# Expert weights read in one 8 KB run per partition, and the expert loop laid out around four plus two PSUM banks

## Chip, cores and metric

The kernel runs on one core of a Trainium2 chip. The metric is the device time of one execution in microseconds (us), lower is better. TensorE (PE) does matrix products, VectorE (DVE) and ScalarE (ACT) elementwise work, GpSimd (POOL) little here, and SyncE (SP) issues the transfers, which 16 DMA engines carry out.

## What is computed

Two transformer blocks over 256 tokens of width 1024 in float32. The change touches only the mixture of experts that ends the first block:

```python
def moe_ffn(h, router_w, router_b, w_mlp1, b_mlp1, w_mlp2, b_mlp2):
    ...
    top_vals, top_idx = lax.top_k(logits, TOP_K)          # 4 of 32 experts for each token
    ...
    def expert_step(acc, params):
        w1, b1, w2, b2, gate_e = params
        u = xt @ w1 + b1                                  # w1 is 1024 x 2048
        glu = jnp.minimum(u[:, ::2], SWIGLU_LIMIT)
        lin = jnp.clip(u[:, 1::2], -SWIGLU_LIMIT, SWIGLU_LIMIT)
        a = glu * jax.nn.sigmoid(SWIGLU_ALPHA * glu) * (lin + 1)
        out = a @ w2 + b2                                 # w2 is 1024 x 1024
        return acc + gate_e[:, None] * out.astype(jnp.float32), None
```

## The kernel before

The first block has its projections, attention and output product, then `rms_modulate`, `route` and `mixture`; the second block (two layers) follows. `route` (L1640) makes a list of work items, each one expert with at most 64 of its tokens (a few with up to 96), on the device. `mixture` (L1853) takes the items two at a time; such a pair i has 128 places, 64 and 64 (`even`) or 96 and 32 (`uneven`). There are 16 pairs in this execution.

**Transfers.** A pair needs 24 pieces of 1 MB, alternately of its two experts: j = 0 to 7 are the first 1024 columns of `w_mlp1`, 8 to 15 the other 1024, 16 to 23 `w_mlp2`. A piece holds 256 rows, two for each partition, 128 rows apart: two runs of 4 KB (`moe_load`, L1632). There are 12 slots (`MOE_SLOTS`): numbers 4 to 7 are the shared weight ring of the whole kernel (`ring`), the others `moe_ring`. SP loads piece j into slot j % 12 as soon as the product that used the slot's last content has added to `halves_done` (L2216 to L2221). The first 12 pieces are loaded ahead, in `rms_modulate` and `route`. When 10 of the last pair's 12 steps are done, SP issues the next stage's first weights (`refill`).

**Products.** `products_of` (L1925) is one step: it waits for two pieces, does 8 calls of a float32 matmul (16 instructions; twice as many of half width for uneven pairs), and adds to `halves_done`. A pair is 12 steps: u for output columns 0 to 1023 in banks 0 and 1 (four steps), u for 1024 to 2047 in the same banks (four), y in the same banks (four). So each bank pair must be emptied before the next bias product (`biases`, L1919) starts it anew: by DVE (`gate`: glu and lin) after the fourth and eighth step, by ACT (copies to `moe_y`) after the twelfth.

**Between the steps** PE also does: `put_back` (L1939), which spreads the last pair's y over the tokens, for DVE to add to the residual (`add_put`); `gather` (L1902), which picks the next pair's tokens out of `turned_h` by the 0/1 matrix `sel`, for ACT to copy to `moe_x`; `turn_hidden` (L1911), which transposes the gated result (128 columns at a time) for ACT to copy to `moe_hid`; and the transpose of `gated`, for ACT to copy to `moe_back`. These use banks 2 and 3 (`misc`, `summed`). Banks 4 to 7 hold the products with b2 at the beginning (`acc`). The order is written by hand: put_first after step 4, put_second after 5, the first two turns after 6, gathers after 8 and 9, the other turns after 10, `gated` after 11. `sigmoid` runs on ACT between `gate` and `multiply` on DVE.

Of the kernel before, what the change touches and what calls it, by code (L numbers as in the profile page):

```python
# [213 lines left out]
class Builder:  # L214
# [1408 lines left out]
    def moe_piece(self, j):  # L1623

        x = j % MOE_SLOTS
        if SHARED <= x < SHARED + SLOTS:
            at = self.ring[:, x - SHARED, :, :]
        else:
            at = self.moe_more[:, x if x < SHARED else x - SLOTS, :, :]
        return at.rearrange("p a b -> p (a b)").rearrange("p (k c) -> p k c", k=2)  # L1630

    def moe_load(self, sp, j, expert):  # L1632

        g, kk = j // 8, j // 2 % 4
        name, c = ("w_mlp1", g) if g < 2 else ("w_mlp2", 0)
        w = self.dram[name][0].rearrange("e (c p) n -> e p c n", p=P)
        src = w[bass.ds(expert, 1), :, 2 * kk:2 * kk + 2, 1024 * c:1024 * c + 1024]
        sp.dma_start(self.moe_piece(j), src.rearrange("e p c n -> (e p) c n")).then_inc(self.moe_landed[j % MOE_SLOTS], 16)
# [214 lines left out]
    def mixture(self, comb_t, b2, ctx):  # L1853
# [16 lines left out]
        glu, lin, sig, act_out = (self.sb(f"moe_{n}", [P, 2, 256], ctx=ctx) for n in ("glu", "lin", "sig", "act"))  # L1870
# [9 lines left out]
        out = self.bank[0:2]  # L1880
        misc = lambda half: self.bank[2 + half][:, 0:S]
        summed = lambda d: self.bank[2 + d // 2 % 2][:, S * (d % 2):S * (d % 2) + S]
# [10 lines left out]
        with self.stage() as block:  # L1893
            @block.tensor
            def _(pe):
# [15 lines left out]
                def turn_hidden(i, q):  # L1911

                    pe.wait_ge(hidden.sem, i * 4 + (q + 1))
                    for j in range(2):
                        mm = nc.tensor.transpose(misc(q % 2)[:, PAIR * j:PAIR * j + PAIR],
                                                 act_out[:, q % 2, P * j:P * j + P], ident)
                    mm.then_inc(turned.sem, 1)

                def biases(g):  # L1919

                    for o in range(2):
                        nc.tensor.matmul(out[o][:, :], row_of[:, 2 * g + o, :], b1, start=True, stop=False,
                                         skip_group_check=True)

                def products_of(i, tiles, g, kk, lhs):  # L1925

                    for m in range(2):
                        j = 8 * g + 2 * kk + m
                        pe.wait_ge(landed[j % slots], i * (16 * chunks // slots) + 16 * (j // slots + 1))
                    for k in (2 * kk, 2 * kk + 1):  # L1930
                        for o in range(2):
                            for c, n_cols, m in tiles:
                                mm = nc.tensor.matmul(out[o][c:c + n_cols, :], lhs[:, k, c:c + n_cols],  # L1933
                                                      self.moe_piece(8 * g + 2 * kk + m)[:, k % 2, 512 * o:512 * o + 512],
                                                      start=(g == 2 and k == 0), stop=(k == KC - 1),
# [10 lines left out]
                def put_first(i):  # L1946

                    put_back(0)
# [23 lines left out]
                def pair(i, tiles, after=True):  # L1972

                    pe.wait_ge(rows_ready.sem, i + 1)
                    taken(i, 0)
                    if after:
                        pe.wait_ge(y_taken.sem, i * 2)
                    biases(0)
                    products_of(i, tiles, 0, 0, x)
                    yield  # L1980
                    for kk in (1, 2, 3):
                        products_of(i, tiles, 0, kk, x)
                        yield
                    if after:
                        put_first(i)
                    pe.wait_ge(lins.sem, i * 4 + 2)
                    biases(1)
                    products_of(i, tiles, 1, 0, x)
                    yield
                    if after:  # L1990
                        put_second(i)
# [1330 lines left out]
```

## Time and profile before

| | us |
|---|---|
| three runs | 2628.89, 2629.95, 2622.94 (median 2628.89) |
| the profiled execution | 2629.03 |
| its span, first to last instruction | 2627.2 |
| PE busy in the span | 2358.1 |
| DVE, ACT, POOL busy | 960.5, 719.2, 136.8 |

The expert loop lies from about 319 to 1294 us of the span, some 37% of it. In the page of the profile, the span is cut into 40 slices of 66 us. A line of the timeline gives the start, the duration, engine, source line, what is written <- what is read, a count, and in brackets how long the engine stood idle before it and for whom. Matmul durations overlap: a group that lasts 1.99 us is followed by the next one 1.92 us after its start. Each float32 matmul call is two records (x16 is 8 calls), a transpose one.

### The profile page before, as it was taken

What the parts mean: (1) busy time and instruction counts of PE and PEld (TensorE: products, weight loads), DVE (VectorE), ACT (ScalarE), POOL (GpSimd) and SP (SyncE); (2) the same over time, 40 slices, a digit from 0 to 9 for tenths busy, and PEclk for the clock granted to TensorE, in tenths of its full rate; (3) what the DMA queues carried; (4) which work ended last, traced back from release to release, by engine and by line L of the source; (5) the groups of instructions that cost most, each with busy time, mean ns of one, the idle gap of its engine ahead of it and who ended that gap; (6) DMA issues with size and microseconds to landing.
All of it is one profiled execution on the core that took longest, in us unless ns stands there. A gap on an engine that the chain in (4) does not pass through costs nothing. (4 is left out here: it accounts for less than half of the span.)

```text
span 2627.2 us, 37215 instructions
## 1 busy us (share of the span) xinstructions
PE 2358.1 (90%) x14984; PEld 1555.3 (59%) x14984; DVE 960.5 (37%) x1779; ACT 719.2 (27%) x1166; POOL 136.8 (5%) x145
## 2 busy tenths in 40 slices
PE   6988899999999999999899977999999989888997
PEld 4966533333333333333498555678787788557997
DVE  2355312111211111111321656654344431756565
ACT  2354211111111111111232544342122242445333
POOL 0100000000000000000000213200000200211000
PEclk9988799999999999999999988999999999989999
DMA  9655699999999999999823433232332223434462
GB/s 288 167 164 181 238 393 404 402 409 403 407 408 406 409 410 410 408 409 409 314 83 109 161 102 107 81 96 61 108 106 71 88 75 125 145 105 134 145 192 83
DMA packets 351334, 605.52 MB, mean 230 GB/s; under 512 B 15056, under 2 KB 251600, under 8 KB 351088
## 3 DMA queue, kind: packets, MB, share of 16 engines
q1 hardware_dynamic: 351216, 603.84, 63.9%
q8 instruction: 88, 1.44, 0.2%
q14 instruction: 30, 0.25, 0.0%
HBM read 602.74 MB, written 1.05 MB: 230 GB/s over the span
## 5 line engine op out<-in xcount | busy, mean ns | idle before, releaser
L1933 PE MATMUL banks<-moe_ring,moe_x 128*64 128x512 f32 (+1 forms) x1920 | 346.9, 597 | 5.5 <-DMA moe_ring<-in_w_mlp 5.4
L2136 DVE TENSOR_SCALAR moe_glu<-banks 128x256 f32<-128x256 f32 x64 | 26.9, 420 | 736.1 <-PE banks L1933 736.1
L1933 PEld LDWEIGHTS banks<-moe_ring,moe_x 128*64 128x64 f32 (+1 forms) x1920 | 104.9, 126 | 223.5 <-issue 223.5
L2533 PE MATMUL banks<-ff_xhi,ff_whi 128*128 128x512 f32 (+1 forms) x672 | 226.5, 337 | 5.5 <-PEq L235 3.9
L2533 PE MATMUL banks<-ff_xhi,ff_wlo 128*128 128x512 f32 (+1 forms) x672 | 226.2, 337 | 0.0
L2533 PE MATMUL banks<-ff_xlo,ff_whi 128*128 128x512 f32 (+1 forms) x672 | 226.1, 337 | 0.0
L529 DVE TENSOR_TENSOR ff_wlo<-ring,ff_whi 128x2048 fp32r<-128x2048 f32 (+2 forms) x76 | 152.7, 2010 | 116.1 <-ACT ff_whi L520 113.9
L803 PE MATMUL banks<-pr_whi,pr_xhi 128*128 128x256 f32 (+1 forms) x640 | 180.4, 282 | 1.2 <-DVE pr_wlo L529 1.2
L803 PE MATMUL banks<-pr_wlo,pr_xhi 128*128 128x256 f32 (+1 forms) x640 | 180.4, 282 | 0.0
L803 PE MATMUL banks<-pr_whi,pr_xlo 128*128 128x256 f32 (+1 forms) x640 | 180.3, 282 | 0.0
L520 ACT CAST ff_whi<-ring 128x2048 fp32r<-128x2048 f32 (+2 forms) x76 | 127.2, 1674 | 149.4 <-PE banks L2588 122.2
L1933 PE MATMUL banks<-ring,moe_x 128*64 128x512 f32 (+1 forms) x640 | 116.3, 596 | 40.0 <-DMA ring<-in_w_mlp 40.0
L529 DVE TENSOR_TENSOR pr_wlo<-ring,pr_whi 128x2048 fp32r<-128x2048 f32 (+1 forms) x34 | 73.7, 2166 | 191.6 <-ACT pr_whi L520 191.6
L2533 PEld LDWEIGHTS banks<-ff_xhi,ff_whi 128*128 128x128 f32 x672 | 127.7, 190 | 19.5 <-issue 4.5
L2533 PEld LDWEIGHTS banks<-ff_xhi,ff_wlo 128*128 128x128 f32 x672 | 127.7, 190 | 13.1
L2533 PEld LDWEIGHTS banks<-ff_xlo,ff_whi 128*128 128x128 f32 x672 | 127.7, 190 | 13.0
L2588 PE MATMUL banks<-ff_hid_hi,ff_whi 128*128 128x512 f32 (+1 forms) x352 | 122.4, 348 | 12.3 <-PEq L235 12.3
L1933 PE MATMUL banks<-moe_ring,moe_hid 128*64 128x512 f32 (+1 forms) x640 | 116.8, 597 | 15.8 <-DMA moe_ring<-in_w_mlp 11.9
L803 PEld LDWEIGHTS banks<-pr_whi,pr_xhi 128*128 128x128 f32 x640 | 123.1, 192 | 3.1 <-issue 1.7
L803 PEld LDWEIGHTS banks<-pr_wlo,pr_xhi 128*128 128x128 f32 x640 | 123.1, 192 | 0.1
L803 PEld LDWEIGHTS banks<-pr_whi,pr_xlo 128*128 128x128 f32 x640 | 123.1, 192 | 0.0
L2588 PE MATMUL banks<-ff_hid_hi,ff_wlo 128*128 128x512 f32 (+1 forms) x352 | 121.1, 344 | 0.0
(466 smaller groups left out, 3916.0 us busy)
## 6 DMA issues: line engine op xcount, KB each, us to landing
moe_ring<-in_w_mlp SPq DMA_DIRECT2D x256, 1024.0 KB, 18.4
ring<-in_w_mlp SPq DMA_DIRECT2D x128, 1024.0 KB, 18.4
ring<-in_w_ada SPq DMA_DIRECT2D x144, 512.0 KB, 4.7
ring<-in_w_ffn_in SPq DMA_DIRECT2D x88, 512.0 KB, 5.2
ring<-in_w_in SPq DMA_DIRECT2D x60, 512.0 KB, 5.3
ring<-in_w_ffn_out SPq DMA_DIRECT2D x48, 384.0 KB, 3.2
ring<-in_w_out SPq DMA_DIRECT2D x24, 512.0 KB, 4.0
ring<-in_w_ffn_out SPq DMA_DIRECT2D x16, 256.0 KB, 3.4
```

Of the source, the lines that this page charges most:

```text
L520: self.nc.scalar.copy(bufs[0][:, x % depth, 0:kn, 0:width], src)\
L529: self.nc.vector.tensor_tensor(bufs[1][:, x % depth, 0:kn, 0:width], src, bufs[0][:, x % depth, 0:kn, 0:width].bitcast(F32), ALU.subtract)\
L803: mm = nc.tensor.matmul(out, a, b, start=(k == 0 and term == 0), stop=(k == KC - 1 and term == 2))
L1933: mm = nc.tensor.matmul(out[o][c:c + n_cols, :], lhs[:, k, c:c + n_cols], self.moe_piece(8 * g + 2 * kk + m)[:, k % 2, 512 * o:512 * o + 512],
L2136: nc.vector.tensor_scalar(glu[:, o, :], u[:, 0, :], SWIGLU_LIMIT, None, ALU.min).then_inc(glus.sem, 1)
L2533: mm = nc.tensor.matmul(self.bank[2 * (f % 4) + side][:, 0:width], w[:, k, :], xp[:, k, :], start=(k == 0 and term == 0), stop=(k == KC - ...
L2588: mm = nc.tensor.matmul(self.bank[d][:, 0:width], w[:, k - k0, :], hp[:, k, :], start=(k == 0 and term == 0), stop=(k == fp - 1 and term = ...
```

## The change

- A piece is one run of 8 KB for each partition. Of `w_mlp1`, piece 2k + m is 128 whole rows (all 2048 columns) of expert m's chunk k. Of `w_mlp2`, a piece is 256 rows, partition p holding rows 2p and 2p + 1 of them; `hid` is then transposed with a stride of two (even, then odd columns). Pieces still are 1 MB, 24 a pair, 12 slots, in the same counts for `halves_done`.
- u has four banks (0 to 3), y two (4 and 5), the rest banks 6 and 7. A pair is eight steps `up` (each over all 2048 columns), then four steps `down`.
- put_first moves to after step 2, put_second to after step 4. All four gathers, the four bias calls of the next pair and the first two turns lie between the eighth step and the ninth; the third turn after the ninth, the fourth after the tenth, `gated` after the eleventh.
- All four `gate`s follow the eighth step on DVE. `glu`, `lin`, `sig` hold four quarters, `act_out` is gone (in place in `lin`). ACT's order is take_x and sigmoid in turn, twice, take_x twice, take_hidden and sigmoid in turn, twice, take_hidden twice.
- At the beginning PE waits for all four copies of x before the last products with b2, and does four bias calls before the first step, not two.

```diff
+        own = bass.ds(expert, 1)
+        if j < 2 * KC:
+            w = self.dram["w_mlp1"][0].rearrange("e (c p) n -> e c p n", p=P)[own, j // 2, :, :]
+        else:
+            w = self.dram["w_mlp2"][0].rearrange("e (c p r) n -> e c p (r n)", p=P, r=2)[own, j // 2 - KC, :, :]
+        sp.dma_start(self.moe_piece(j), w.rearrange("e p n -> (e p) n")).then_inc(self.moe_landed[j % MOE_SLOTS], 16)
...
+        u_bank, y_bank = self.bank[0:4], self.bank[4:6]
+        misc = lambda half: self.bank[6 + half][:, 0:S]
+        summed = lambda d: self.bank[6 + d // 2 % 2][:, S * (d % 2):S * (d % 2) + S]
...
+                def biases(i, after=True):
+                    pe.wait_ge(rows_ready.sem, i + 2 if after else 1)
+                    for o in range(4):
+                        if after:
+                            pe.wait_ge(lins.sem, i * 4 + (o + 1))
+                        nc.tensor.matmul(u_bank[o][:, :], row_of[:, o, :], b1, start=True, stop=False, skip_group_check=True)
...
+                def up(i, tiles, k):
+                    step_landed(i, k)
+                    for o in range(4):
+                        for c, n_cols, m in tiles:
+                            mm = nc.tensor.matmul(u_bank[o][c:c + n_cols, :], x[:, k, c:c + n_cols],
+                                                  self.moe_piece(2 * k + m)[:, 512 * o:512 * o + 512],
+                                                  start=False, stop=(k == KC - 1), skip_group_check=True)
+                    mm.then_inc(halves_done.sem, 1)
...
                 def put_first(i):
+                    taken(i, 0)
+                    pe.wait_ge(y_taken.sem, i * 2)
                     put_back(0)
                     put_back(2)
...
+                pe.wait_ge(turned_taken.sem, 4)
                 for d in range(4, KC):
...
+                    for k in range(KC):
+                        up(i, tiles, k)
+                        if after and k == 1:
+                            put_first(i)
+                        if after and k == 3:
+                            put_second(i)
                     pe.wait_ge(sel_ready.sem, i + 2)
+                    for g in range(4):
+                        if g < 2:
+                            pe.wait_ge(put_added.sem, i * 4 + (3 + g))
+                        else:
+                            taken(i, g - 1)
                         gather(g)
+                    taken(i, 3)
+                    turn_hidden(i, 0)
+                    biases(i)
+                    taken(i, 4)
+                    turn_hidden(i, 1)
+                    for q in range(4):
+                        taken(i, 5 + q)
+                        down(i, tiles, q)
+                        if q < 2:
+                            turn_hidden(i, 2 + q)
+                        if q == 2:
+                            for t in range(2):
+                                mm = nc.tensor.transpose(misc(0)[:, P * t:P * t + P], gated[:, t, :], ident)
+                            mm.then_inc(turned.sem, 1)
...
+                    for q in range(2):
+                        take_x(i, q)
+                        sigmoid(i, q)
+                    for q in range(2):
+                        take_x(i, 2 + q)
+                    for q in range(2):
+                        take_hidden(i, q)
+                        sigmoid(i, 2 + q)
+                    for q in range(2):
+                        take_hidden(i, 2 + q)
...
+                    gate(i, 0)
+                    for q in range(4):
+                        times_linear(i, q)
+                        if q < 3:
+                            gate(i, q + 1)
+                        times_sigmoid(i, q)
```

## Rows read from the trace of the kernel before

**Rows 1.** The page: GB/s moved in 40 slices of the span, and packet sizes.
```profile
GB/s 288 167 164 181 238 393 404 402 409 403 407 408 406 409 410 410 408 409 409 314 83 109 161 102 107 81 96 61 108 106 71 88 75 125 145 105 134 145 192 83
DMA packets 351334, 605.52 MB, mean 230 GB/s; under 512 B 15056, under 2 KB 251600, under 8 KB 351088
```
**Rows 2.** Busy time by window, expert loop: PE, PEld, DVE, ACT, POOL, clock, DMA share, GB/s.
```profile
1000.00:1100.00 100.00, 93.00 (x436) 38.87 (x432) 22.16 (x68) 10.55 (x26) 0.00 (x0) 1.00 1.02 408
```
**Rows 3.** Timeline of PE, expert loop: four first bias groups, each beginning a pair.
```profile
373.59 1.98 PE L1922 MATMUL banks<-vecs,moe_row_of 128*128 128x512 f32 x4 [1.17 <-ACT moe_y L2091]
...
430.45 1.99 PE L1922 MATMUL banks<-vecs,moe_row_of 128*128 128x512 f32 x4 [1.19 <-ACT moe_y L2091]
...
864.77 1.99 PE L1922 MATMUL banks<-vecs,moe_row_of 128*128 128x512 f32 x4 [1.16 <-ACT moe_y L2091]
...
1233.85 1.99 PE L1922 MATMUL banks<-vecs,moe_row_of 128*128 128x512 f32 x4 [1.16 <-ACT moe_y L2091]
```
**Rows 4.** Timeline of PE in one late pair: each kind of work between the steps.
```profile
1008.70 1.88 PE L1922 MATMUL banks<-vecs,moe_row_of 128*128 128x512 f32 x4
...
1014.10 1.99 PE L1942 MATMUL banks<-moe_back,moe_y 128*128 128x256 f32 x8
1016.02 3.65 PE L1933 MATMUL banks<-moe_ring,moe_x 128*64 128x512 f32 x16
1019.61 0.66 PE L1915 MATMUL banks<-tables,moe_act 128*128 128x128 f32 x4
...
1027.35 2.05 PE L1906 MATMUL banks<-moe_sel,moe_turned_h 128*128 128x128 f32 x16
...
1042.97 0.44 PE L2020 MATMUL banks<-tables,moe_gated 128*128 128x128 f32 x2
1044.25 3.65 PE L1933 MATMUL banks<-moe_ring,moe_hid 128*64 128x512 f32 x16 [0.84 <-DMA moe_ring<-in_w_mlp]
...
1059.62 3.65 PE L1933 MATMUL banks<-ring,moe_x 128*64 128x512 f32 x16 [1.48 <-DMA ring<-in_w_mlp]
```
**Rows 5.** Busy time by window near the start of the span.
```profile
3.00:7.00 4.00, 0.00 (x0) 0.00 (x0) 0.00 (x0) 0.00 (x0) 0.00 (x0) 1.00 1.01 412
...
3.20:7.20 4.00, 0.00 (x0) 0.00 (x0) 0.00 (x0) 0.00 (x0) 0.00 (x0) 1.00 1.03 424
...
14.00:16.00 2.00, 1.98 (x17) 0.71 (x17) 0.00 (x0) 0.00 (x0) 0.00 (x0) 1.00 1.10 349
```
**Rows 6.** The page, DMA issues: two transfers that fill 3 to 7 us.
```profile
tables<-in_tables SPq DMA_DIRECT2D x1, 1136.0 KB, 6.8
...
vecs<-in_vecs SPq DMA_DIRECT2D x1, 817.0 KB, 4.4
```
**Rows 7.** Timelines of ACT, PE and SP as the expert loop begins.
```profile
316.98 0.37 ACT L2046 COPY moe_x<-banks 128x256 f32<-128x256 f32 x1 [0.52 <-PE banks L1906]
317.37 1.28 ACT L2051 ACT_TABLE_LOAD   x1
...
316.87 2.05 PE L1964 MATMUL banks<-moe_comb_t,moe_b 32*128 32x128 f32 x16
318.85 1.99 PE L1922 MATMUL banks<-vecs,moe_row_of 128*128 128x512 f32 x4
...
324.46 4.45 SPq L1638 DMA_DIRECT2D moe_ring<-in_w_mlp  x4
```
**Rows 8.** Timelines of PE and SP as the expert loop ends.
```profile
1290.60 3.65 PE L1933 MATMUL banks<-moe_ring,moe_hid 128*64 128x512 f32 x16 [0.82 <-DMA moe_ring<-in_w_mlp]
...
1284.96 10.03 SPq L392 DMA_DIRECT2D ring<-in_w_in  x8
```
**Rows 9.** Timeline of DVE at a gate, two instructions that follow each other.
```profile
1089.34 0.42 DVE L2136 TENSOR_SCALAR moe_glu<-banks 128x256 f32<-128x256 f32 x1 [10.82 <-PE banks L1933]
1089.68 0.41 DVE L2137 TENSOR_SCALAR moe_lin<-banks 128x256 f32<-128x256 f32 x1
```
**Rows 10.** GB/s in 40 slices of 1.5 us, from 430.45 and from 926.22 us.
```profile
GB/s 401 412 412 404 412 410 407 412 401 363 243 371 423 423 412 423 407 407 415 401 418 410 401 421 404 407 415 401 418 410 401 421 404 407 415 401 421 407 399 421
...
GB/s 415 410 401 423 399 410 418 399 418 399 401 421 401 423 404 410 415 401 418 407 404 418 404 407 418 401 415 410 404 415 407 410 415 404 412 410 404 415 407 407
```

More of the change, by code:

```diff
@@ L1931, in products_of, with down @@
+                def down(i, tiles, q):
+                    step_landed(i, KC + q)
+                    for r in range(2):
                         for o in range(2):
                             for c, n_cols, m in tiles:
-                                mm = nc.tensor.matmul(out[o][c:c + n_cols, :], lhs[:, k, c:c + n_cols],
-                                                      self.moe_piece(8 * g + 2 * kk + m)[:, k % 2, 512 * o:512 * o + 512],
-                                                      start=(g == 2 and k == 0), stop=(k == KC - 1),
+                                at = D * r + 512 * o
+                                mm = nc.tensor.matmul(y_bank[o][c:c + n_cols, :], hid[:, 2 * q + r, c:c + n_cols],
+                                                      self.moe_piece(2 * KC + 2 * q + m)[:, at:at + 512],
+                                                      start=(q == 0 and r == 0), stop=(q == 3 and r == 1),
@@ L1986, in pair @@
[L1986 to L1991, printed above, removed]
-                    products_of(i, tiles, 1, 1, x)
-                    yield
-                    for half in range(2):
-                        pe.wait_ge(put_added.sem, i * 4 + (3 + half))
-                        turn_hidden(i, half)
-                    products_of(i, tiles, 1, 2, x)
@@ L2011, in pair @@
-                    products_of(i, tiles, 2, 1, hid)
-                    yield
-                    for half in range(2):
-                        taken(i, 5 + half)
-                        turn_hidden(i, 2 + half)
-                    taken(i, 7)
-                    products_of(i, tiles, 2, 2, hid)
-                    yield
-                    for t in range(2):
-                        mm = nc.tensor.transpose(misc(0)[:, P * t:P * t + P], gated[:, t, :], ident)
-                    mm.then_inc(turned.sem, 1)
@@ L2035, in _ @@
-                taken(n, 0)
-                pe.wait_ge(y_taken.sem, n * 2)
+                    pair(i, even)
                 put_first(n)
@@ L2090, in pair @@
                     for c in range(2):
-                        nc.scalar.copy(y[:, 512 * c:512 * c + 512], out[c][:, :]).then_inc(y_taken.sem, 1)
-                    yield
-                for g in range(4):
-                    act.wait_ge(turned.sem, g + 1)
-                    take(x[:, 2 * g:2 * g + 2, :], g % 2)
-                with act.Fori(0, n) as i:
-                    for _ in pair(i):
-                        pass
+                        nc.scalar.copy(y[:, 512 * c:512 * c + 512], y_bank[c][:, :]).then_inc(y_taken.sem, 1)
             @block.vector
```

161 lines of the change are left out of this document (40 added, 121 removed).

## The prediction

> **What bounds the kernel now.** I read the page first, for the stretch that the change touches. From the sixth slice to the nineteenth the transfers move 393 to 410 GB/s, and nowhere else nearly as much [rows 1]. That flat top is the expert loop. The window view of 100 us inside it says the same from the engine's side: PE busy 93%, DVE 22%, ACT 11%, the granted clock at its full level (1.00, which is 2.4 GHz), and the 16 DMA engines occupied without a gap (share 1.02, 408 GB/s) [rows 2]. Two resources are close to their limit, so I asked which one waits for the other. In the timeline of PE a late pair has waits for DMA of 0.84 and 1.48 us [rows 4]; the DMA engines wait for nobody. So the loop is bound by the transfers, with PE a few per cent behind.
>
> How far behind decides what a faster transfer can be worth. Six late pairs, from 864.77 to 1233.85, take 61.51 us each; pair 1, from 373.59 to 430.45, still lives on the 12 pieces loaded ahead, hardly waits for data, and takes 56.9 us [rows 3]. The sum of PE's own work agrees. I take each group by the distance to the next start, about 0.07 us less than its duration [rows 4]: 12 steps of 3.59 us are 43.1; two put groups of 1.92 are 3.8; two groups of turns of 0.59 are 1.2; two groups of gathers of 1.98 are 4.0; two bias groups (two calls each) of 1.85 are 3.7; gated is 0.4. That is 56.2 us, plus 1.16 for ACT's copy of y [rows 3] and some tenths for other copies. PE could follow transfers that are 7% faster, not more.
>
> **The packet, the term that matters.** A pair is 24 pieces; each puts 8 partitions x 2 runs = 16 packets of 4 KB on each of the 16 engines, so 384 in 61.51 us: 160.2 ns a packet. The change makes them 192 packets of 8 KB for the same bytes. What does 8 KB cost? Three places of the trace bound it.
> - Packets of 1 KB (the modulation weights at 14 to 16 us, 256 columns of float32) run at 349 GB/s [rows 5], and 16 x 1024 B / 349 GB/s is 46.9 ns. A line through 1 KB and 4 KB: 3072 B more cost 113.3 ns, 27.1 B/ns, with a fixed part of 46.9 - 37.8 = 9.1 ns. By it 8 KB costs 311.3 ns, 421 GB/s.
> - The only long runs in the kernel are `tables` (1136 KB over 128 partitions, 9088 B each) and `vecs` (6.5 KB each) [rows 6]. That such a run stays one packet can be counted: 351334 - 351088 = 246 packets of 8 KB and more [rows 1], enough for the 128 rows of `tables`. They fill 3.2 to 7.2 us at 424 GB/s; the window 3 to 7, with the ramp in it, has 412 [rows 5]. 424 makes 309.1 ns of 8 KB, 412 makes 318.1.
> - No saving is 320.4 ns.
>
> I take 311.3, the line, since it lies between the two readings of the long runs and close to the cleaner one. After the first 12 pieces 372 are streamed, 372 x 8 = 2976 packets of 8 KB per engine, each 320.4 - 311.3 = 9.1 ns cheaper: **-27.1 us** (ends: -33.6 by 424, -6.8 by 412, 0 by no saving).
>
> The Trainium skill (DMA: Bandwidth & Descriptors, Why small descriptors are slow) puts the fixed part at about 3 cycles beside one cycle for each 32 bytes, and says that joining descriptors pays only up to 256 bytes. By its cycle of 32 B at the port rate (850 MHz) that is 3.5 ns and not 9.1, an estimate of 10.5 us saved in the place of 27.1. Its table on the same page has 425 GB/s for a very long transfer, which lies beside the 424 of rows 5. The trace bears more on the second.
>
> **Stalls that I leave as they are.** The stream from 324.46 [rows 7] to the last piece at 1290.60 [rows 8] takes 966.1 us, while 15.5 pairs at 61.51 are 953.4. The 12.7 us between are dips: in the pair from 430.45 the rate falls to 363, 243, 371 GB/s for three slices some 15 us into it, and in the pair from 926.22 it does not [rows 10]. Nothing in the trace names their cause. They stand in the sum at zero change; the bounds are -12.7 (gone) and +12.7 (doubled).
>
> **The start.** PE now waits for the last copy of x (316.98 + 0.37 = 317.35) ahead of the b2 products that began at 316.87 [rows 7]: +0.5. Four bias calls stand before the first step and not two: +1.9. The first slot is freed, and the stream starts, 2.4 us later than 324.46: **+2.4**, all of it on the path, for nothing is in flight then.
>
> **The hole between up and down.** After the eighth step PE does four gathers (4.0), two turns (0.6) and four bias calls (3.7): 8.3 us of work without a piece used. Beside it DVE has 16 instructions. Independent ones follow each other at 0.34 us, one that needs the last result at 0.42 and a little [rows 9]: gate 0 is done at 0.8 us, the first hidden quarter about 2.5 if sigmoid is in time. It isn't quite: the ACT table load of 1.28 us, once a pair, stands ahead of the first sigmoid [rows 7], and that sigmoid now follows take_x(0) (PE 1.0, copy 0.4). So sigmoid 0 ends near 3.2, take_x(1) near 3.5, the fourth gather starts 0.5 us late. All lins are there by 6 us, the last bias call comes at about 7.8; the second hidden quarter at 5, its turn at 8.5. I find one wait, 0.5 us: the hole is **8.8 us**. The stride of two in the turns has no row; at nothing or at double their 1.2 us a pair it is covered, as PE keeps 3 us a pair in hand.
>
> A pair for PE: 8 x 3.59 + 3.8 + 8.8 + 4 x 3.59 + 0.6 + 0.4 = 56.7 us. The copy of y (1.16 us of wait before [rows 3]) now lies beside steps 1 and 2. A pair for the transfers: 192 x 311.3 ns = 59.8 us. Transfers remain the bound. Can the hole starve them? A slot has 6 steps, 29.9 us, from landing to the landing of what follows in it; the ninth step's end lags its landing by about 11 us, so at least six pieces stay queued. Cost zero; if PE were ever 25 us behind, the stream would stop.
>
> **The end.** Here the hole does cost. The transfers land two pieces every 16 x 311.3 ns = 4.98 us. Counted from the landing for step eight, the last pair lands after 19.9 us, and PE needs 3.6 + 8.8 + 14.4 + 1.0 = 27.8: it ends 7.9 us after the last piece, where before it needed only the one step, 3.6 [rows 8]. **+4.3**. The issue of the next stage's weights moves from 5.6 us before the last landing [rows 8] to about the landing; some 10 us to move them, with PE's own tail of 7.9 us and the put group beside them: covered, with a bound of +2.
>
> **Sum**: -27.1 + 2.4 + 4.3 = -20.4 us. The profiled execution took 2629.0, of it 2627.2 span; it becomes 2608.6, and as the median of the runs is 0.1 lower, 2608.5.
>
> **Rivals.**
> - *The run length gives little.* The 412 of the wider window, or 320.4 ns a packet, or an 8 KB run that is split again. Against it speak the 246 long packets and the 424; for it, that 4 us of stream is little evidence. At 412: -6.8 + 2.4 + 3.8 = -0.6, so 2628. At no saving: +2.4 + 3.7, 2635. The page's 3 cycles end between this and my sum: -10.5 + 6.7, 2625. Chance 0.20, of which 0.05 for the page's figure.
> - *The stalls go too.* They come near pieces 6 to 9, about where reading passes from the first half of the rows to the second; whole rows have no such jump. Against it: other jumps (to `w_mlp2`, to the next experts) show none. -12.7 more: 2596. Chance 0.15.
> - *PE's hole becomes the bound; slower.* Place: between the eighth and ninth step. If gates, sigmoids, copies and turns don't overlap the gathers and biases, the 16 DVE instructions (7 us) add to the 8.3 us of work: hole 15.3, pair 63.2. PE then sets the loop: 319.3 + 16 x 63.2 - 3.8 = 1327, 33 us behind the 1294.2 of before: 2662. It decides above a pair of 61.2 us, a hole of 13.3. Against it speaks the schedule above. Chance 0.08.
> - My forecast: 0.57.
>
> **How the numbers follow.** The likeliest is 2608.5. The range goes from 2588 (424 GB/s and no stalls, -33.6 - 12.7 + 6.7) to 2633, almost the case of no saving. Outside lie the hole and the edge of the first rival, under 0.2. A measurement of this kernel tells about 0.3% (8 us) from no change. Faster than 2621: my case and the vanished stalls, with 0.02 of the first rival, 0.74. Within: 0.18. Slower than 2637: 0.08, the hole.
>
> **What would show it.** Packets near 302,000 in all (98,304 of 4 KB become 49,152 of 8 KB); GB/s in the flat slices 418 to 424; late pairs 59.5 to 60.5 us apart; PE's waits for DMA at the last ups of a pair only, none at downs; the gap from the eighth to the ninth step near 8.8 us with a wait of half a microsecond; PE ending about 8 us after the last piece. Wrong it would be if the rate stays at 408 with the long packets, if dips grow, or if PE never waits for DMA.

## The result, and the profile after

| | before | after |
|---|---|---|
| median of the runs, us | 2629.07 (2622.94 to 2631.48) | 2600.18 (2594.77 to 2607.75) |
| ratio | | 0.9897, 95% interval 0.9871 to 0.9923 |
| the profiled execution, us | 2629.03 | 2600.18 |
| its span | 2627.2 | 2598.4 |

The change takes 28.9 us off, where 20.4 were forecast: 2600.2 and not 2608.5. The direction and the range held. The page of the changed kernel, the same two lines as in [rows 1]:

```profile
GB/s 291 162 162 194 229 410 421 422 421 421 421 422 422 422 422 422 422 422 422 220 60 143 170 86 94 81 97 67 120 92 69 83 83 124 133 114 130 152 187 84
DMA packets 302182, 605.52 MB, mean 233 GB/s; under 512 B 15056, under 2 KB 251600, under 8 KB 252784
```

The same bytes in 302,182 packets in place of 351,334, and a top that is both higher (421 to 422 where it was 402 to 410) and flatter. The flatness is what the forecast did not have. A window of 100 us in the loop, against [rows 2] (PE, PEld, DVE, ACT, POOL, granted clock, DMA share, GB/s):

```profile
1000.00:1100.00 100.00, 95.48 (x444) 39.93 (x442) 18.17 (x54) 16.04 (x34) 0.00 (x0) 1.00 1.01 422
```

PE's timeline: the start of the loop, the end of step eight and the hole behind it in a late pair, and the last pair. To be held against [rows 7], [rows 4] and [rows 8].

```profile
315.76 2.05 PE L1984 MATMUL banks<-moe_comb_t,moe_b 32*128 32x128 f32 x16 [0.46 <-ACT moe_x L2038]
317.74 3.70 PE L1926 MATMUL banks<-vecs,moe_row_of 128*128 128x512 f32 x8
...
353.82 3.60 PE L1926 MATMUL banks<-vecs,moe_row_of 128*128 128x512 f32 x8
...
409.71 3.60 PE L1926 MATMUL banks<-vecs,moe_row_of 128*128 128x512 f32 x8
...
875.87 3.65 PE L1938 MATMUL banks<-moe_ring,moe_x 128*64 128x512 f32 x16 [1.33 <-DMA moe_ring<-in_w_mlp]
879.46 2.94 PE L1907 MATMUL banks<-moe_sel,moe_turned_h 128*128 128x128 f32 x24
883.07 1.16 PE L1907 MATMUL banks<-moe_sel,moe_turned_h 128*128 128x128 f32 x8 [0.66 <-ACT moe_x L2038]
...
884.30 3.60 PE L1926 MATMUL banks<-vecs,moe_row_of 128*128 128x512 f32 x8
...
888.05 3.65 PE L1950 MATMUL banks<-ring,moe_hid 128*64 128x512 f32 x16
...
1233.80 3.65 PE L1938 MATMUL banks<-moe_ring,moe_x 128*64 128x512 f32 x16 [1.32 <-DMA moe_ring<-in_w_mlp]
...
1242.22 3.60 PE L1926 MATMUL banks<-vecs,moe_row_of 128*128 128x512 f32 x8
...
1257.97 3.65 PE L1950 MATMUL banks<-moe_ring,moe_hid 128*64 128x512 f32 x16
```

The bias products mark the pairs. From 884.30 to 1242.22 there are six: 59.65 us a pair, 310.7 ns for a packet of 8 KB. Pair 1 (353.82 to 409.71) doesn't live on the stream yet and takes 55.9 us. So the transfers still set the pace, PE stands 6% behind, and its waits for data are at the last steps of `up`, as forecast. The hole from 879.46 to 888.05, where the ninth step begins, is 8.6 us long, with one wait of 0.66.

What ACT does in the hole is the schedule that the prediction worked out, the table load ahead of the first sigmoid:

```profile
880.65 0.37 ACT L2038 COPY moe_x<-banks 128x256 f32<-128x256 f32 x1 [34.21 <-PE banks L1907]
881.04 1.28 ACT L2043 ACT_TABLE_LOAD   x1
882.34 0.42 ACT L2043 ACTIVATE moe_sig<-moe_glu 128x256 f32<-128x256 f32 x1
882.66 0.35 ACT L2038 COPY moe_x<-banks 128x256 f32<-128x256 f32 x1
882.91 0.42 ACT L2043 ACTIVATE moe_sig<-moe_glu 128x256 f32<-128x256 f32 x1
```

### The profile page after: what moved, and what is told of

It reads as the page before. It is cut to its first block and busy times, and to the rows that moved or that the text cites. A ratio compares the mean times of both kernels' runs of the same rounds, so it can differ in the third digit from the quotient of the medians.

```text
span 2598.4 us, 37215 instructions
## 1 busy us (share of the span) xinstructions
PE 2356.1 (91%) x14992; PEld 1563.3 (60%) x14992; DVE 962.8 (37%) x1779; ACT 737.2 (28%) x1182; POOL 136.0 (5%) x145
## 2 busy tenths in 40 slices
DMA packets 302182, 605.52 MB, mean 233 GB/s; under 512 B 15056, under 2 KB 251600, under 8 KB 252784
## 3 DMA queue, kind: packets, MB, share of 16 engines
HBM read 602.74 MB, written 1.05 MB: 232 GB/s over the span
## 5 line engine op out<-in xcount | busy, mean ns | idle before, releaser
L1938 PEld LDWEIGHTS banks<-moe_ring,moe_x 128*64 128x64 f32 (+1 forms) x1920 | 110.2, 126 | 266.3 <-issue 266.3
L2127 DVE SCALAR_TENSOR_TENSOR res<-banks,mod,res 128x256 f32<-128x256 f32 x136 | 59.4, 479 | 467.0 <-PE banks L1959 457.5
L2038 ACT COPY moe_x<-banks 128x256 f32<-128x256 f32 x68 | 24.9, 366 | 566.5 <-PE banks L1907 566.5
L2551 PE MATMUL banks<-ff_hid_lo,ff_whi 128*128 128x512 f32 (+1 forms) x352 | 120.3, 342 | 0.0
```

What stands on the lines that cost most here:

```text
L1938: mm = nc.tensor.matmul(u_bank[o][c:c + n_cols, :], x[:, k, c:c + n_cols], self.moe_piece(2 * k + m)[:, 512 * o:512 * o + 512], start=Fals ...
L2038: nc.scalar.copy(dst, misc(half).rearrange("p (k c) -> p k c", k=2)).then_inc(turned_taken.sem, 1)
L2127: return nc.vector.scalar_tensor_tensor(r, source, self.mod[:, 5, d, 0:1], r, ALU.mult, ALU.add)
L2551: mm = nc.tensor.matmul(self.bank[d][:, 0:width], w[:, k - k0, :], hp[:, k, :], start=(k == 0 and term == 0), stop=(k == fp - 1 and term = ...
```

## Where the time went

"The loop" is from here on the time from the start of the first bias product to the end of the last step: 975.3 us before, 943.8 after. It begins 1.1 us earlier (317.74 against 318.85). So PE is done 32.6 us earlier (1261.6 against 1294.2), and this splits up as follows, with the sum's own terms beside it.

| | forecast | measured |
|---|---|---|
| packets: 15.5 pairs, 59.65 and not 61.51 us | -27.1 | -28.8 |
| stalls in the stream | 0 | -8.6 |
| the stream's start | +2.4 | +0.5 |
| PE's tail behind the last piece: 7.9 and not 3.6 us | +4.3 | +4.3 |
| PE's end of the loop | -20.4 | -32.6 |
| behind the loop | 0 | +3.8 |

The stalls: the stream starts at about 324.97 (3.60 after the first step's 321.37), and the last piece lands 19.9 us after the landing for step eight (1233.80), at 1253.7. That is 928.7 us, and 15.5 pairs are 924.6: 4.1 us left, where 12.7 were left before. The 40 slices of 1.5 us from 430.45, which in [rows 10] held 363, 243, 371:

```profile
GB/s 426 410 421 426 431 415 421 415 426 426 431 415 421 415 421 431 421 426 410 415 426 437 421 415 415 421 426 426 431 415 410 426 426 426 421 415 421 421 421 437
```

Not all of the 8.6 are these dips. The stream also comes up to its rate sooner. First the kernel before, 40 slices from 324.46, then the changed kernel, 40 slices from 320:

```profile
GB/s 25 287 344 320 232 284 421 421 423 412 407 407 418 410 410 412 401 412 415 410 410 399 410 412 410 396 412 418 412 407 410 407 404 415 412 404 412 396 276 254
```
```profile
GB/s 0 11 0 0 235 431 421 421 426 426 437 426 437 421 404 421 426 426 437 421 404 421 410 426 437 421 404 421 426 426 437 421 404 415 426 426 421 431 415 399
```

In its first 15 us the stream of before moves 4.75 MB, which is 3.4 us less than 410 GB/s would give, and that of the changed kernel 5.65 MB, 1.6 us less than 422 GB/s would give. So 1.8 us of the 8.6 lie at the start, which leaves 6.8 for the dips of the pairs (two experiments below find 7.3 and 7.4). And most of the 4.1 that are left lie at the two ends: 1.6 there, and 1.9 in the last 2.7 us before the landing, in which only 0.35 MB are moved.

The start's +0.5 is the +2.4 of the prediction, less 1.9 us by which the routing ahead of the loop happened to be done sooner. The 3.8 us lost behind the loop have nothing to do with the change's code. The same instruction of the last part of the block stands 33.9 us earlier than before. First the timeline of POOL in the kernel before, then after:

```profile
2094.30 0.30 POOL L3222 MEMSET gl_wa<- 32x256 f32 x1 [0.62 <-POOLq L235]
```
```profile
2060.41 0.30 POOL L3185 MEMSET gl_wa<- 32x256 f32 x1 [0.62 <-POOLq L235]
```

The end of the span is only 28.8 us earlier. Between lies a stretch with a lower granted clock in the second execution; the windows that answer to each other, before and after (the last three columns are the granted clock, DMA share and GB/s):

```profile
2250.00:2300.00 50.00, 42.68 (x366) 28.20 (x366) 39.55 (x83) 24.33 (x46) 16.42 (x15) 0.91 0.46 148
2300.00:2360.00 60.00, 50.31 (x526) 32.83 (x526) 29.48 (x64) 29.23 (x50) 8.92 (x12) 0.85 0.32 106
```
```profile
2216.00:2266.00 50.00, 42.52 (x340) 27.38 (x340) 35.13 (x80) 22.99 (x42) 12.69 (x12) 0.86 0.45 148
2266.00:2331.00 65.00, 54.88 (x551) 36.46 (x551) 32.92 (x67) 30.95 (x54) 12.27 (x14) 0.82 0.32 99
```

This differs from one execution to the next: the same kernel once more has the same loop and a span of 2591.2 (f4_after_again below). So the experiments are compared by the loop in the trace (943.8 and 943.7 us for the same kernel) and by the interval of the ratio where there is one.

## The experiments

Two things changed at once: the transfers (longer runs, whole rows) and the order of the loop. The theory was the prediction's own, that run length alone brings the gain and that the new loop costs some 6 us; against it stood that the new order takes part in the gain, as the vanished dips suggested.

### The old loop with the new transfers

```diff
-        src = w[bass.ds(expert, 1), :, 2 * kk:2 * kk + 2, 1024 * c:1024 * c + 1024]
+        if j < 2 * KC:
+            w = self.dram["w_mlp1"][0].rearrange("e (c p) n -> e c p n", p=P)[own, j // 2, :, :]
+        else:
+            w = self.dram["w_mlp2"][0].rearrange("e (c p r) n -> e c p (r n)", p=P, r=2)[own, j // 2 - KC, :, :]
```

> The loop of before, with the transfers of after: every piece is whole rows, one run of 8 KB for each partition. Nothing else is changed, so the products take the wrong weights (the columns and rows are not where this loop looks for them), and only the time is read. Theory A, the run length and the addresses are all that matters, and the new loop order itself costs time: 422 GB/s and late pairs of 59.66 us as in after, no dips, and the end and start of the old loop (3.6 us after the last piece instead of 7.9, stream starts 2.4 us earlier): 2600.2 - 6.7 = 2593.5 us. Theory B, the dips belong to the order of the old loop (banks, puts, gates) and went because that went: pairs of 59.7 late, but dips of some 9 us in the first eight pairs stay: 2602 us. If the old loop's PE work (56.9 us in a pair without data waits) were the limit, pairs of 57 to 58 us would show no wait for DMA.

Measured: median 2587.6, ratio to before 0.9864 (0.9842 to 0.9886), loop 937.9 us. Its page:

```profile
GB/s 291 163 163 196 230 361 421 422 421 422 421 422 422 422 422 422 422 422 422 271 76 119 173 105 99 69 96 69 114 101 68 88 76 127 147 114 131 155 186 84
```

The old order gets the same 59.65 us a pair and the same flat top. The whole gain is in the transfers, the dips included; the new order costs 5.9 us beside it (943.8 against 937.9), which is near the +6.7 that the prediction gave for start and end. The new order is what makes whole rows usable, since a whole row fills four banks at once. It is the price of the run length and not a gain.

### The new loop with the old transfers

```diff
+        g, kk = j // 8, j // 2 % 4
+        name, c = ("w_mlp1", g) if g < 2 else ("w_mlp2", 0)
+        w = self.dram[name][0].rearrange("e (c p) n -> e p c n", p=P)
+        src = w[bass.ds(expert, 1), :, 2 * kk:2 * kk + 2, 1024 * c:1024 * c + 1024]
```

> The loop of after, with the transfers of before: pieces of two half rows, two runs of 4 KB for each partition, column half after column half (so again the products take wrong weights, and only the time is read). Theory A: 160.2 ns a packet and late pairs of 61.5 us as before, dips near pieces 8 and 9 in the early pairs (12.7 us in all), and the new loop's costs on top (+2.4 at the start, +4.3 at the end): 2629 + 6.7 = 2635.7 us, slower than before. Theory B, dips belong to the old loop order: late pairs of 61.5, no dips: 2627 us.

Measured: 2632.2, ratio 1.0034 (1.0018 to 1.0049), loop 979.2, pairs of 61.7 us late in it. GB/s in 40 slices of 1.5 us, from 411 us:

```profile
GB/s 407 410 412 407 418 393 412 410 407 415 404 404 407 410 415 407 404 415 407 412 407 410 412 303 298 404 429 423 412 421 410 399 415 410 401 418 404 412 418 396
```

The dip (303 298) is there. It goes with the transfers and not with the order of the work. The loop is 3.9 us longer than before's: that is the new order's price with short runs. It was expected to be 6.7, and it is 5.9 with long runs; a part may be that the dips are smaller here (303 and 298 against 363, 243 and 371), which isn't shown.

### Whole rows, short runs

The changed kernel, with each piece as two transfers of 1024 columns: the addresses of whole rows, in runs of 4 KB, and twice as many transfers.

```diff
-        sp.dma_start(self.moe_piece(j), w.rearrange("e p n -> (e p) n")).then_inc(self.moe_landed[j % MOE_SLOTS], 16)
+        piece, w = self.moe_piece(j), w.rearrange("e p n -> (e p) n")
+        for c in (0, D):
+            sp.dma_start(piece[:, c:c + D], w[:, c:c + D]).then_inc(self.moe_landed[j % MOE_SLOTS], 16)
```

> After, but each piece comes as two transfers of 512 KB, one for each half of the 8 KB run, so as runs of 4 KB from the same addresses in nearly the same order; the result is the same. Packet theory: 160.2 ns a packet again, late pairs of 61.5 to 62 us, GB/s 405 to 410. For the dips: if they come with any 4 KB packets, they are back (some 12 us, 2636 us in all); if they come with reading one column half of all rows and then the other, they stay away (2625 us). If the rate stays at 422, the packet length is not what pays, but the place from which is read.

Measured, in one run: 2628.4, loop 971.9, a pair 61.44 us. Its page:

```profile
GB/s 289 166 154 192 226 388 409 410 409 410 409 410 410 410 410 409 410 410 410 303 83 109 161 103 106 81 96 61 108 107 70 88 74 126 145 105 134 145 192 83
DMA packets 357479, 605.56 MB, mean 231 GB/s; under 512 B 21200, under 2 KB 257744, under 8 KB 357232
```

And its slices of 1.5 us from 411 us, where the kernel before this one fell to 303 298:

```profile
GB/s 415 410 410 407 412 410 401 410 410 410 404 410 404 412 407 404 418 407 410 412 404 418 404 412 410 407 412 410 404 418 404 412 410 407 415 407 407 412 407 412
```

This run separates the two effects. A packet of 4 KB costs 61.44 us / 384 = 160.0 ns, beside 160.2 before, though there are twice as many transfers: their number costs nothing that shows. And the dips are gone. So from before to after the loop goes 975.3, +3.9 (new order), -7.3 (whole rows: no dips), -28.1 (run length; 320.0 - 310.7 = 9.3 ns by 2976 packets are 27.7), to 943.8.

Here the Trainium skill can be weighed (DMA: Bandwidth & Descriptors, Why small descriptors are slow). Its overhead of about 3 cycles a packet, 3.5 ns, would have made the last of these steps an estimated 10.5 us. It is 28.1, and the measurement decides.

### The same number of transfers, runs left at 8 KB

Meant as the control to the last one: each piece as two transfers of 64 partitions.

```diff
+        for p in (0, P // 2):
+            sp.dma_start(piece[p:p + P // 2, :], w[p:p + P // 2, :]).then_inc(self.moe_landed[j % MOE_SLOTS], 16)
```

> After, but each piece comes as two transfers of 64 partitions, 512 KB each, with whole runs of 8 KB; the result is the same. It is the control of the run with column halves: the same number of transfers, but packets of 8 KB. Packet theory: 421 GB/s, late pairs of 59.7 to 60 us, some 2600 to 2604 us. If the number of transfers or what ends each of them has a price of its own, it shows here: each 0.1 us for a transfer would be 24 x 0.1 = 2.4 us a pair.

Measured, in one run: 3408.4, the loop's pairs 112.6 us. A window of 100 us in it:

```profile
800.00:900.00 100.00, 64.82 (x312) 24.72 (x314) 11.37 (x34) 8.04 (x17) 0.00 (x0) 0.81 1.02 225
```

The expectation was 421 GB/s. The DMA engines are occupied without a gap (share 1.02) and move 225 GB/s, so each packet of 8 KB takes 586 ns and not 311. As a control it failed; the one before has to serve, since there twice the transfers left the packet at its 160 ns. What halves the rate can't be read from this trace: it was tried at this one size only.

### One of the two matrices alone

The kernel before, with only the pieces of `w_mlp2` as 8 KB runs and the turns of `hid` at a stride of two.

```diff
+        if g == 2:
+            w2 = self.dram["w_mlp2"][0].rearrange("e (c p r) n -> e c p (r n)", p=P, r=2)[bass.ds(expert, 1), kk, :, :]
...
+                    halves = act_out[:, q % 2, :].rearrange("p (c r) -> p r c", r=2)
```

> Before, with one part of the change alone: w_mlp2's pieces as one run of 8 KB (rows 2p and 2p + 1) and the turns of the hidden rows with a stride of two; w_mlp1 and the loop stay; the result the same. Packet theory: 1024 of the 2976 long packets an engine, each 9.7 ns cheaper than two of 4 KB: 9.9 us less than before, 0.38%; late pairs 60.9 us. The turns should cost nothing that shows. If the dips come from reading w_mlp1 by column halves, they stay, all of them; if w_mlp2's two distant rows had a part in them, they shrink.

Measured: 2620.3, ratio 0.9973 (0.9957 to 0.9989), loop 965.5, 9.8 shorter than before's; a late pair 60.88 us. GB/s from 430 us in slices of 1.5 us:

```profile
GB/s 401 410 421 396 415 399 289 257 328 412 423 418 418 410 415 407 410 412 415 418 429 426 426 421 415 421 426 426 421 426 421 407 418 401 412 404 412 410 407 418
```

In one line lie both rates: about 410 for 4 KB, then some twelve slices around 424 while `w_mlp2` streams, then 410 again. A third of the long runs brings a third of the gain, and the dip stays. The stride of two in the turns costs nothing that the loop shows.

### Where the dips come from

The rival of the prediction put them where reading passes from the first half of the rows' columns to the second, which is also where it jumps back from the last rows to the first. Two kernels made from before test that, with `w_mlp1` read in another order. In the first, the two column halves alternate every 256 rows:

```diff
+        if g < 2:
+            kk, c = j // 4, j // 2 % 2
```

> Before, with the pieces of w_mlp1 fetched in another order: for each 256 rows first the one half of the columns, then the other, and then the next rows; all runs still 4 KB, two distant rows in a piece. The products take the wrong weights; only the time is read. If the dips come from the jump back from the last rows to the first (once a pair, near pieces 8 and 9), they are gone, and all pairs take 61.4 to 61.5 us: about 12 us less than before in the loop. If they come from reading half rows as such, dips stay, spread or as large as before.

Measured, in one run: 2635.8, loop 978.3, late pairs 61.46. From 373.5 us, where before has one dip:

```profile
GB/s 412 371 352 429 418 412 421 295 281 273 393 423 421 415 418 314 251 317 399 423 421 418 415 404 410 412 410 401 418 401 410 415 404 410 410 410 412 404 412 410
```

Three dips, though this kernel never jumps back to the first rows. In the second kernel the pieces of the second half read the first half of the columns again, so that the jump back to the first row stays and only the half doesn't change:

```diff
-        name, c = ("w_mlp1", g) if g < 2 else ("w_mlp2", 0)
+        name, c = ("w_mlp1", 0) if g < 2 else ("w_mlp2", 0)
```

> Before, except that the pieces for the second half of w_mlp1's columns read the first half again: the same runs of 4 KB, the same order of rows and the same jump back from the last rows to the first, but no change of the half. The products take wrong weights; only the time is read. If the dips come from changing over from one half of the rows' 8 KB to the other, they are gone, all pairs from the second on take 61.4 to 61.5 us. If they come from the jump back in rows, they stay in the first eight pairs.

Measured, in one run: 2616.1, loop 967.9, 7.4 less than before's. From the start of the stream (324 us), and from 430.45:

```profile
GB/s 8 194 360 325 227 249 388 426 421 421 412 412 399 415 412 407 415 404 412 410 401 418 396 415 412 407 407 407 412 410 410 412 407 407 412 407 410 410 399 410
...
GB/s 415 407 407 410 410 410 404 415 415 407 407 410 410 412 401 415 415 407 407 410 410 410 404 415 415 407 407 410 410 412 401 412 418 407 407 410 410 412 401 415
```

The dips of the pairs are gone, with runs of 4 KB and the old order. So the jump back in the rows alone doesn't make them. Their price is nearly the same by both ways: 7.4 us here, 7.3 for whole rows in the new order. The one at the start of the stream (227 249) stays.

But the change of the column half alone doesn't make them either. The kernel with the halves in turn changes the half seven times in `w_mlp1` of each pair, and has three dips. Where they lie can be counted by the bytes moved since the stream began with piece 12 of pair 0, at 1.05 MB a piece: 17.99 MB from 328 to 375 us, 21.57 to 384 and 25.95 to 396, just as the rate falls, are pieces 5, 8 and 12 of pair 1. In the kernel before it is piece 8 (21.71 MB from 325 to 381 us). So the dips come soon after pieces 4, 8 and 12, at which the half changes and reading also goes on to the next 256 rows; after pieces 2, 6, 10 and 14, at which the half changes within the same rows, no dip begins. And the run with each piece as two transfers by column changes the half with every transfer, and has no dip.

What these runs show is this: the dips go when `w_mlp1` is read in whole rows, or when only one half is read, and each dip that was located begins where half and rows change together. No run here makes a rule of that. The kernel that reads one half twice also fetches the same bytes twice, which the others don't. What in the memory or in the path does it, and why late pairs don't show it, remains open.

### The ends of the loop

The changed kernel again, unchanged, for the comparison:

> The changed kernel once more, unaltered, on the chip of the runs beside it, so that they can be set against it. The ratio measured at first was 0.9897 [0.9871, 0.9923]; the loop is bound by transfers at one rate, so the same again within that interval, and late pairs of 59.66 us.

Measured: 2594.9, ratio 0.9883 (0.9864 to 0.9903), span 2591.2, loop 943.7, a pair 59.65.

Then an attempt at the +4.3 and at the start: the products with b2 ahead of the gathers, and a last pair without the gathers and bias products whose results nobody uses (a tiny product stands in for each gather).

```diff
+                        if last:
+                            nc.tensor.matmul(misc(g % 2)[:, 0:1], self.turned_h[:, 0, 0:P], sel[:, 0, 0:1], start=True, stop=True)\
+                                .then_inc(turned.sem, 1)
...
+                    if not last:
+                        biases(i)
```

> After, with the two ends of the loop shortened, the result the same. At the start the last b2 products stand ahead of the gathers (in PE's wait of 3.0 us for sel), the first gathers use banks 0 and 1, and the first bias calls follow at once: the first step should start 2.9 us earlier. In the last pair the four gathers and four bias calls, which nobody uses, are left out (one tiny product stands for each gather): the hole there is then set by gate, sigmoid and copies, some 4.3 us instead of 8.6, and PE should end 3.6 us and not 7.9 after the last piece. Theory (both costs lie on the path): 7.2 us less than after, 0.27%. Rival (the end is covered by the next stage's weights, which are issued late and have to land first): PE ends earlier but the next stage's first product doesn't, and only 2.9 us are gained.

Measured: 2600.8, ratio 0.9897 (0.9875 to 0.9919), loop 943.3. The hole did become short, and nothing came of it. The timeline of PE and the windows of hole and following step:

```profile
1246.17 0.61 PE L2011 MATMUL banks<-moe_sel,moe_turned_h 128*128 128x1 f32 x4
...
1249.01 0.38 PE L2011 MATMUL banks<-moe_sel,moe_turned_h 128*128 128x1 f32 x2 [1.61 <-ACT moe_x L2049]
...
1251.31 6.37 PE L1955 MATMUL banks<-ring,moe_hid 128*64 128x512 f32 x16
```
```profile
1246.00:1251.00 5.00, 2.35 (x14) 1.75 (x12) 4.05 (x12) 3.88 (x9) 0.00 (x0) 0.90 1.03 428
1251.00:1258.00 7.00, 7.00 (x20) 2.03 (x18) 1.65 (x5) 0.69 (x2) 0.00 (x0) 0.58 1.01 418
```

The hole is 5.1 us, but the step behind it takes 6.37 us in the place of 3.65: the granted clock is 0.58 of full speed over these 7 us, so mostly at the lower level of 1.2 GHz. PE had worked for 2.35 of the 5 us ahead of it. In the changed kernel PE works for 7.93 of the 8.60 us of the same hole (1237.40 to 1246.00), and the clock stays at 1.00 there. So the work taken out had kept the clock up, as far as one execution of each tells.

At the start nothing was gained either, but for another reason. Timeline and window:

```profile
316.92 3.77 PE L1983 MATMUL banks<-moe_comb_t,moe_b 32*128 32x128 f32 x16 [2.91 <-issue]
```
```profile
310.00:317.00 7.00, 4.09 (x21) 3.57 (x19) 1.69 (x14) 0.00 (x0) 0.00 (x0) 0.50 0.29 121
```

PE stood idle for 2.91 us ahead of the moved b2 products all the same, so they didn't fill the wait. And they took 3.77 us and not 2.05, at a clock of 0.50, which is 1.2 GHz. That clock isn't the edit's doing: it stood at 0.50 before them, from 310 us on, and in the same 7 us it is 0.50 in the profiled executions of the old loop with the new transfers and of the 16 KB runs as well.

So the next one takes out less: the gathers stay, only the last pair's bias products go.

```diff
-                    biases(i)
+                    if not last:
+                        biases(i)
...
+                with pe.Fori(n_last, n) as i:
+                    pair(i, even, last=True)
```

> After, with only the four bias calls left out in the last pair (nobody uses them), the gathers kept, the start as in after; the result the same. The run with short ends lost its gain to the granted TensorE clock: its PE had 2.35 us of work in 5 us, and the clock in the next 7 us was 0.58. If the clock holds here, as the gathers keep PE busy, the hole of the last pair is 8.6 - 3.4 = 5.2 to 5.6 us and PE ends 4.6 to 5 us after the last piece, 3 us less than after. If even this lighter hole lowers the clock, the first step after it takes more than 3.6 us.

Measured: 2595.7, ratio 0.9896 (0.9872 to 0.9919), loop 941.0. Timeline and window of its last hole:

```profile
1235.42 2.94 PE L1910 MATMUL banks<-moe_sel,moe_turned_h 128*128 128x128 f32 x24
1239.03 1.16 PE L1910 MATMUL banks<-moe_sel,moe_turned_h 128*128 128x128 f32 x8 [0.66 <-ACT moe_x L2044]
...
1241.13 3.65 PE L1953 MATMUL banks<-ring,moe_hid 128*64 128x512 f32 x16
```
```profile
1233.00:1242.00 9.00, 8.04 (x52) 5.30 (x50) 5.03 (x15) 4.56 (x11) 0.00 (x0) 1.00 1.01 422
```

The hole is 5.7 us, PE works for 4.74 of them (1235.40 to 1241.10), the clock stays at 1.00, and PE ends 24.9 us after the landing for step eight and not 27.8: 2.9 us, which the loop shows (2.8). The ratio can't show so little.

### Runs of 16 KB

The changed kernel with transfers of 2 MB, two rows of `w_mlp1` or four of `w_mlp2` for each partition. The slots come free four pieces at a time.

```diff
-            w = self.dram["w_mlp1"][0].rearrange("e (c p) n -> e c p n", p=P)[own, j // 2, :, :]
+            w = self.dram["w_mlp1"][0].rearrange("e (c p r) n -> e c p (r n)", p=P, r=2)[own, q, :, :]
...
-            w = self.dram["w_mlp2"][0].rearrange("e (c p r) n -> e c p (r n)", p=P, r=2)[own, j // 2 - KC, :, :]
+            w = self.dram["w_mlp2"][0].rearrange("e (c p r) n -> e c p (r n)", p=P, r=4)[own, q - KC // 2, :, :]
```

> After, with runs of 16 KB, the result the same: two pieces of one expert come as one transfer of 2 MB into two neighbouring slots (two whole rows of w_mlp1, four of w_mlp2 for each partition); gathers pick every second feature, turns every fourth hidden column, and a turn waits for two quarters. Slots come free in groups of four pieces, after two steps. Packet theory (a fixed 9.3 ns and 27.2 B/ns, fitted to 160.0 ns for 4 KB and 310.7 ns for 8 KB): 612 ns for 16 KB, 428 GB/s, late pairs of 58.8 us, still above PE's own 55.9: 15.5 x 0.86 = 13 us less in the stream, but 3.6 us more before the first slot is freed and 3.7 us more at the end, since the last landing releases two steps and not one: some 6 us less than after, 2594 or a ratio to before of about 0.986. Rival: above 8 KB the packet is cut or the rate has met another limit, and late pairs stay at 59.66: then it is 7 us slower than after.

Measured: 2591.2, ratio 0.9865 (0.9842 to 0.9888), loop 940.6, a pair 58.73. The packets of its page:

```profile
DMA packets 274534, 605.50 MB, mean 233 GB/s; under 512 B 11985, under 2 KB 248529, under 8 KB 249713
```

And a window of 100 us in the loop:

```profile
800.00:900.00 100.00, 94.12 (x438) 40.71 (x436) 22.92 (x68) 12.81 (x28) 0.00 (x0) 1.00 1.01 429
```

A packet of 16 KB takes 58.73 us / 96 = 611.8 ns. The line through 4 KB (160.0) and 8 KB (310.7) says 612.1. So from 4 to 16 KB a packet costs 9.3 ns and 1 ns for each 27.2 bytes.

The stream did what was expected, the loop did not quite: it is 3.2 us shorter than after's, and 6 were expected. Of the 2.8 missing, 1.7 are the clock of this execution at the start: the first bias calls took 5.40 us in the place of 3.70. The other 1.1 are not accounted for.

```profile
325.71 5.40 PE L1936 MATMUL banks<-vecs,moe_row_of 128*128 128x512 f32 x8
```

### Both together

16 KB runs and the last pair without bias products.

```diff
+                with pe.Fori(n_last, n) as i:
+                    pair(i, even, last=True)
```

> The two edits that paid in the traces, together: runs of 16 KB, and no bias calls in the last pair; the result the same. The stream's rate (58.73 us a pair) and the shorter last hole act in different places, so they add: 6 us less than after from the one, 2.9 from the other, a ratio to before of 0.984 to 0.985. If the first turn's wait for two hidden quarters is what ends the last hole once the bias calls are gone (hidden 2 comes near 5 us after the last up), the second edit brings 2.4 and not 2.9.

Measured: 2591.2, ratio 0.9861 (0.9839 to 0.9884), loop 935.9, the shortest of all and 7.9 us under after's, where 8.9 were expected, or 8.4 if the second hidden quarter ends the hole. It is 4.7 us under the 16 KB runs alone, but 1.7 of that is the slow start of that kernel's execution. Its lowest run is 2580.4, but the intervals of this kernel, of the 16 KB runs alone and of the changed kernel overlap. By the loop it is the best; end to end that isn't shown.

## Why the prediction was right, and where it was off

- **What bounds the kernel: right.** The transfers did before and do after. PE's own pair, forecast at 56.7 us, takes 55.9, and the old loop with the new transfers has the same pair as the new one.
- **The packet: right, 1.7 us short.** The line through 1 KB and 4 KB gave 311.3 ns; it is 310.7. On its side stood the 424 GB/s of the 4 us with `tables` and `vecs` [rows 5, 6], and the 412 of the wider window was indeed the ramp. The 0.6 ns by 2976 packets are the difference.
- **Stalls left at zero change: the step that failed.** The term was set to 0 with 12.7 as its bound, and measured -8.6. With it the forecast would have been 2599.9, though that it lands so near is luck: the packet's 1.7, the routing's 1.9 and the 3.8 behind the loop nearly cancel there. The rival that names it (2596) was given 0.15 and ends 4 us from the result, nearer than the forecast's 8.3. The argument against it was that other jumps show no dip. That compared unlike things: neither the jump to `w_mlp2` nor that to the next experts goes back over the same matrix for the other half of its rows. The rival had the right place and the right cure, whole rows; the cause stays open, since the change of the half alone gives no dip (four of seven changes, and every change in the run with column halves). And it claimed all 12.7, while 4.1 are there with whole rows too.
- **The start: right in kind.** PE waited 0.46 for ACT's copy (0.5 forecast), and four bias calls take 3.6 us, 1.7 to 1.9 more than two. The routing's 1.9 us hid it in this execution.
- **The hole: right.** 8.6 us for 8.8; one wait, 0.66 for 0.5, behind the table load.
- **The end: right.** 7.9 us behind the last piece, as worked out, and the refill moved to the last landing, as SP's timeline has it:

```profile
1253.69 7.01 SPq L392 DMA_DIRECT2D ring<-in_w_in  x8
```

  The next stage's first product comes 10.5 us after the last put group begins, 10.8 before, so nothing waits for it.
- **What the sum can't hold**: 3.8 us given back behind the loop, by the clock of one execution. Where that didn't happen, in the repeated kernel, the medians lie 33.6 us apart (2628.6 and 2594.9), which is close to the loop's 32.6.
- **A slip in the range.** Its lower end is given as 2588, but -33.6 - 12.7 + 6.7 is -39.6, which makes 2589.4. The result lies inside either way.

## What to carry to other kernels

When the DMA engines are busy without a gap, count packets and not transfers: two packet sizes in the same trace already give the fixed part of a packet, and what longer runs save is that part times the packets that go. That held here for transfers over all 128 partitions; over 64 it did not. Look for slices where a flat stream falls, ask which addresses change there, and price them as a term of their own. And before work is taken out of a short hole of TensorE, look at the granted clock behind it.

## What the runs showed that was not expected

- Two transfers of 64 partitions each, back to back, run at 225 GB/s, where one of 128 partitions with the same runs of 8 KB has 422, and two by column half have 410.
- A stream of 4 KB runs falls to between 243 and 371 GB/s for two or three slices of 1.5 us where it passes to the other half of 8 KB rows and to other rows at once, in the first pairs and not in late ones; 7.3 to 7.4 us in this loop. Four changes of the half within the same rows had no dip.
- 5 us in which PE works 2.35 are followed by 7 us at a clock of 0.58, while a hole of 5.7 us in which it works 4.74 keeps 1.00. Cutting more work cost what it saved.
- Runs of 16 KB bring 428 to 429 GB/s, still on the same line: 9.3 ns and 27.2 bytes a nanosecond.
